# A two-model transformer chain in float32 by split weights: the rows of x handed from block to block in halves, with GpSimd multiplying them by their norm

## What is computed

```python
def first_block(...):
    for l in range(DEPTH):
        mod = cs @ w_ada[l] + b_ada[l]
        h = rmsnorm(x, g_pre[l]) * (1.0 + scale) + shift
        y = hybrid_mixer(h, w_in[l], w_out[l], ...)
        x = x + gate * rmsnorm(y, g_post[l])
def second_block(...):
    for i in range(DEPTH):
        h = _modulate(x, sh_a, sc_a)
        m = _neighborhood_attention(h, ...) if i % 2 == 0 else _mla(h, ...)
        x = x + g_a[:, None, :] * m
        h = _modulate(x, sh_f, sc_f)
        f = _swiglu(h, ...) if i % 2 == 0 else _moe(h, ...)
        x = x + g_f[:, None, :] * f
    return _rmsnorm(x) * final_norm
```

## Time and profile before

| | |
|---|---|
| median of 3 runs | 1661.28 us (1660.46 to 1663.12) |
| profiled execution, device time | 1663.32 us |
| its span in the profile | 1661.5 us, 21232 instructions |
| TensorE matmuls busy | 1427.0 us (86%) |
| VectorE busy | 1216.3 us (73%) |
| ScalarE busy | 862.0 us (52%) |
| GpSimd busy | 65.6 us (4%) |
| chain that ended last | TensorE 53%, VectorE 27%, ScalarE 9% |

### The profile page before, as it was taken

How to read it: one execution, slowest core, us unless ns; L and a number is a source line. 1 busy time by engine, 2 the same in 40 slices (tenths; PEclk the granted TensorE clock), 3 DMA queues, 4 the chain that set the end, 5 groups by cost and what they waited for, 6 DMA issues and landing times.

```text
span 1661.5 us, 21232 instructions
## 1 busy us (share of the span) xinstructions
PE 1427.0 (86%) x7628; PEld 1191.2 (72%) x7628; DVE 1216.3 (73%) x1484; ACT 862.0 (52%) x1210; POOL 65.6 (4%) x82
## 2 busy tenths in 40 slices
PE   2799986999869976899986796999999999999993
PEld 1688676886758845899985685877777777777772
DVE  8667556866565655788785645789889888899895
ACT  0444444444434434233433554577777777776772
POOL 0000000000010000000000102100000000000001
PEclk9989898998989979899997897899999999999996
DMA  9764423735236632678774203699899999999782
GB/s 397 298 249 147 159 101 142 277 142 189 77 143 250 240 128 76 250 279 302 283 276 143 96 38 136 252 350 366 339 347 368 345 349 374 329 365 356 287 371 89
DMA packets 61537, 403.08 MB, mean 243 GB/s; under 512 B 6534, under 2 KB 9734, under 8 KB 15116
## 3 DMA queue, kind: packets, MB, share of 16 engines
q1 hardware_dynamic: 52416, 379.45, 60.3%
q10 hardware_dynamic: 7020, 15.17, 2.6%
q0 software_dynamic: 2016, 7.34, 1.2%
HBM read 393.01 MB, written 8.91 MB: 242 GB/s over the span
## 4 chain that ended last, share of the span: by engine, by line
PE 53%; DVE 27%; ACT 9%; issue 7%; DMA 2%; POOL 1%; ACTq 0%; DVEq 0%; SPq 0%; POOLq 0%
DVE w_lo L2177 16%; PE PS L826 14%; PE PS L828 13%; PE PS L827 13%; ACT w_hi L1602 4%; ACT xg L1696 2%; DVE acc L2194 2%; PE PS L998 1%; PE PS L978 1%; DMA raw<-in_ws 1%; DVE a_lo L2337 1%; DVE hb L2346 1%; DVE hb L2348 1%; PE PS L1251 1%; PE PS L896 1%
## 5 line engine op out<-in xcount | busy, mean ns | idle before, releaser
L2177 DVE TENSOR_TENSOR w_lo<-raw,w_hi 128x2048 fp32r<-128x2048 f32 x287 | 659.6, 2298 | 160.8 <-ACT w_hi L1602 138.3
L1602 ACT ACTIVATE w_hi<-raw 128x2048 fp32r<-128x2048 f32 x287 | 547.8, 1919 | 234.9 <-PE PS L828 222.2
L826 PE MATMUL PS<-w_hi,h_hi 128*128 128x512 f32 (+2 forms) x812 | 340.2, 419 | 28.6 <-DVE h_lo L2598 8.9
L827 PE MATMUL PS<-w_lo,h_hi 128*128 128x512 f32 (+2 forms) x812 | 321.3, 396 | 0.0
L828 PE MATMUL PS<-w_hi,h_lo 128*128 128x512 f32 (+2 forms) x812 | 321.2, 396 | 0.0
L826 PE MATMUL PS<-h_hi,w_hi 128*128 128x256 f32 x776 | 232.3, 299 | 21.4 <-DVE h_lo L2222 11.4
L827 PE MATMUL PS<-h_lo,w_hi 128*128 128x256 f32 x776 | 224.3, 289 | 0.0
L828 PE MATMUL PS<-h_hi,w_lo 128*128 128x256 f32 x776 | 224.1, 289 | 0.0
L826 PEld LDWEIGHTS PS<-w_hi,h_hi 128*128 128x128 f32 x812 | 157.9, 194 | 73.8 <-DVE w_lo L2177 15.7
L2194 DVE SCALAR_TENSOR_TENSOR acc<-raw,cs,acc 128x512 f32<-128x512 f32 x252 | 189.5, 752 | 8.9
L828 PEld LDWEIGHTS PS<-w_hi,h_lo 128*128 128x128 f32 x812 | 157.7, 194 | 33.7
(11 more groups left out here) (310 smaller groups left out, 1444.9 us busy)
## 6 DMA issues: line engine op xcount, KB each, us to landing
raw<-in_ws SPq DMA_DIRECT2D x359, 1024.0 KB, 5.6
y_rows<-ysb ACTq DMA_DIRECT2D x10, 512.0 KB, 7.4
rp<-in_rp ACTq DMA_DIRECT2D x8, 384.0 KB, 4.7
ckb<-in_ck ACTq DMA_DIRECT2D x2, 1024.0 KB, 4.9
y_rows<-ones ACTq DMA_DIRECT2D x3, 512.0 KB, 8.6
x<-in_x SPq DMA_DIRECT2D x1, 1024.0 KB, 11.6
gpost<-in_gpost ACTq DMA_DIRECT2D x2, 512.0 KB, 5.2
x_rows<-xn_f ACTq DMA_DIRECT2D x2, 512.0 KB, 3.8
```

Source lines behind the costliest of these rows:

```text
L826: t.matmul(out, lhs[0], rhs[0], start=start, stop=False, skip_group_check=True)
L827: t.matmul(out, lhs[0], rhs[1], start=False, stop=False, skip_group_check=True)
L1602: a.activation(wh[:, SPL_AT[e.phase][i], :], raw[:, r, :], ACT.Copy).then_inc(*e.inc("hi"))
L2177: v.tensor_tensor(wl[:, s, :], raw[:, r, :], wh[:, s, :].bitcast(F32), ALU.subtract).then_inc(*e.inc("raw_used"))
```

## The change

**Halves.** `turn` works on one half. A new function `first_sums` on TensorE does, for half 0 and then for half 1, the transposes and all sums of the first slot of that half; it is used in `lay0`, `lay1`, `na` and `mla`. In `ffn` only the transposes are by halves. ScalarE's and VectorE's `norm` treat half 0 to the end before half 1, with hb in two parts: VectorE scales the first 4 feature tiles of a half, ScalarE the other 4. The update of x at the end of a phase becomes part of the next phase's `norm` (`lay_update`, `sums_update`), so it stands behind that phase's first w_hi and w_lo.

**GpSimd.** It makes the inverse root of each half by itself and then multiplies that half of x by it (`normed`); VectorE's multiplications are gone.

**Order.** So that a first slot can be summed by halves of tokens, the MoBA values become slot 0 of a layer, and the rest move back by one; four slots stand ahead of the ticks now and four in them. `turn_y(0, 1, 5)` moves into `out_moba(0)`. `cmp_out` moves behind `turn_probs`. In `na` the w_ada blocks end before the last two weight blocks, two filling pieces stand ahead of `scores(0)`, and the output sums run in another order, as in `mla` before. In `ffn`, `down` goes by halves, and `ada(11)` stands ahead of the last one.

```diff
-LAY_FILL = [(1, 2) if i % 4 == 3 and i < 16 else (1, 1) for i in range(18)] + [(0, 0)] * (LAY_TICKS - 18)
+LAY_FILL = [(1, 1)] * 14 + [(0, 1)] * 4 + [(0, 0)] * (LAY_TICKS - 18)
-LAY_ADA = {8: 2, 9: 3, 11: 4, 14: 5}
+LAY_ADA = {9: 2, 10: 3, 12: 4, 15: 5}
-NA_FILL = [(1, 2)] * 8 + [(0, 0)] * (NA_TICKS - 8)
-NA_OUT = {10: 1, 11: 1, 12: 1, 13: 1, 14: 1, 15: 1, 16: 2}
+NA_AHEAD = 2
+NA_FILL = [(1, 2)] * 6 + [(1, 1)] * 2 + [(0, 0)] * (NA_TICKS - 8)
+NA_OUT = {9: 1, 10: 1, 11: 1, 12: 1, 13: 1, 14: 1, 15: 2, 16: 2}
...
+            def normed(xn, m):
+                pool.wait_ge(*e.last("rstd"))
+                g.tensor_scalar(xn[:, m, :], x[:, m, :], st[:, s_rs + m:s_rs + m + 1], None,
+                                ALU.mult).then_inc(*e.inc("xn"))
...
+            for p in ("lay0", "lay1", "na"):
+                e.enter(p)
+                for m in range(MT):
+                    if p != "lay0":
+                        rstd(2 * m + 1, [(2 + m, 3 + m, D)])
+                    rstd(m + 1 if p == "lay0" else 2 * m + 2, [(m, m + 1, D)])
+                    normed(xn_n if p == "na" else xn_l, m)
...
+            def turn(src, m):
+                pe.wait_ge(*e.at("xn", m + 1))
...
+            def first_sums(src, banks, width, m0_done=None):
+                for m in range(MT):
+                    turn(src, m)
...
+                    for kh in range(2):
+                        pe.wait_ge(*e.at("hi", kh + 1))
+                        pe.wait_ge(*e.at("h_hi", 2 * m + kh + 1))
...
                     for c in range(2):
+                        if m == 0 and c == 1:
+                            pe.wait_ge(*e.at("y", 4))
+                            turn_y(0, 1, 5)
...
+                if posted:
+                    y_square(xn, 0)
+                square(xn, 0)
+                hi_to(2)
+                if posted:
+                    y_square(xn, 1)
+                elif e.phase != "lay0":
+                    square(xn, 1)
+                if ahead:
+                    ahead()
+                hi(0, 0)
+                scaled(0)
+                hi(0, 1)
+                if posted or e.phase == "lay0":
+                    square(xn, 1)
+                hi_to(SPL)
+                hi(1, 0)
                 scaled(1)
+                hi(1, 1)
...
+                updated(0)
+                if posted:
+                    scaled(0)
+                    updated(1, (0,))
+                    lo(0, 0)
+                    updated(1, (1,))
+                    lo(0, 1)
+                    split_to(2)
...
+                scaled(1)
+                lo(1, 0)
+                lo(1, 1)
+                split_to(SPL)
```

More of the change, by code:

```diff
@@ L62, in lay_steps_before @@
     out = sum(n for t, n in LAY_OUT.items() if t < tick)
-    return 6 + pieces // 4 + (out >= 6) + (out >= 8)
+    return 8 + pieces // 4 + (out >= 6) + (out >= 8)
 def lay_slots_before(tick):
@@ new lines, in out_sums @@
+                def out_sums():
+                    pe.wait_ge(*e.at("h", 5))
+                    for c in range(2):
+                        yield from out_piece(0, 0, c)
+                    pe.wait_ge(*e.at("h", 6))
+                    yield from out_piece(0, 1, 0)
+                    pe.wait_ge(*e.at("h", 7))
+                    for c in range(2):
+                        yield from out_piece(1, 0, c)
+                    yield from out_piece(0, 1, 1)
+                    pe.wait_ge(*e.at("h", 8))
+                    for c in range(2):
+                        yield from out_piece(1, 1, c)
@@ L1318, in neighbourhood @@
                 ada(0)
-                for b in LAY_BANK[0:6]:
+                fill, out = projections(), out_sums()
+                for _ in range(NA_AHEAD):
+                    next(fill)
+                for b in LAY_BANK[1:6]:
                     pe.wait_ge(*e.at(f"bank{b}", 1))
                 scores(0)
-                fill, out = projections(), out_first()
                 for i in range(NA_TICKS):
@@ L1366, in neighbourhood @@
                         values(i - 1)
-                out_second(0)
-                pe.wait_ge(*e.at("o_used", 4))
-                turn_o(1, 5)
-                out_second(1)
+                next(out)
+                turn_o(3, 5)
+                for _ in out:
+                    pass
             neighbourhood()
@@ L2012, in _ @@
             start("ffn")
-            squares(xn_f)
-            get_brow(4)
-            h_hi()
+            norm(xn_f, ahead=lambda: get_brow(4))
             ffn()
```

504 lines of the change are left out of this document (228 added, 276 removed).

## The result

The changed kernel takes 1666.8 us (median of 6 runs, 1661.9 to 1669.7), the kernel before 1661.8 in the same runs: ratio 1.0029, 95% interval 1.0017 to 1.0042.

The account below looks back on a forecast made before the run. TensorE was taken to idle in hand-over chains and in gaps inside blocks. Hand-overs -8.2, layers -4 and neighbourhood attention -10.3 sum to -22.5 us: 1640.8 profiled, 1639 against the median, stated as 1640, range 1627 to 1657.

Parts of the forecast that it names:

- The unknown price: GpSimd's multiply of 128x1024 elements by a column of scalars: taken as 1.5 us, ends 1.0 and 4.75.
- The hand-overs: Five passages between blocks: first layer +0.6, layer 1 -4.9, neighbourhood -4.9, FFN +1, latent attention 0; together -8.2 us.
- the 1.7 us of the transposes: Last transposes of y inside out_moba(0): its 1.48 us wait goes and out_moba(1) ends 1.7 us earlier.
- rival (a): Hand-overs: TensorE stays at its lower clock for both first halves, leaving 4.3 us of gain, 1657; chance 0.13.
- 2.3 comes back: Into the FFN: 20.4 us against 17.0, but w_lo number 1 stood behind it before, so the net loss is 1 us.
- half 1 waits for half 0's sums and ends about where both ended before: Into the latent attention: half 0's first matmul at 898.5 against 902.38, half 1's end unchanged, so 0 us.
- Inside the blocks: Layers: cmp_out's move -4 us; neighbourhood attention: filling pieces, w_ada order, transposes and clock, less 3 lost, -10.3 us.
- -4 for cmp_out: In each layer, a filling piece and transposes now fill the gap ahead of cmp_out: 2.0 us gained each.
- Rival (b): Gaps inside the blocks come back elsewhere; only the hand-overs and the transposes count: 1652 us, chance 0.14.
- (c): GpSimd's multiply costs 4.75 us at about eight places in the hand-over chains: 1665, slower; decides from 4.3; chance 0.09.
- (d): Hand-overs: half 1's chain is so long that half 0 only waits earlier: 1659 to 1663 us, chance 0.07.
- What would show it: Trace signs: multiply 1.3 to 2 us; wrong if multiplies exceed 4, clock low through both halves, or new gaps between ticks.

Follow-up runs that it names:

- dve_a: Changed kernel with VectorE instead of GpSimd multiplying both halves, half 1 behind w_lo: 1649.9 us, ratio 0.9920 to the kernel before.
- ffn_lo: Changed kernel with VectorE multiplying, half 1 ahead of w_lo, but into the FFN w_lo number 1 behind both halves: 1652.2 us, ratio 0.9938 to the kernel before.
- undo_both: Changed kernel with cmp_out back at the head of ticks 6 and 7 and ada(11) behind the last down projection: 1668.6 us, ratio 1.0045 to the kernel before.
- the second execution: Profiled execution of the changed kernel run once more, unchanged: 1666.6 us profiled, median of that run 1667.2 us.
- before_turny: Kernel before with only the last transposes of y moved between the column halves of out_moba(0) in both layers: 1661.6 us, ratio 1.0004.

## Why the prediction was wrong

*The view of what bounds the kernel* was right: the hand-overs are chains that TensorE waits for, and what lengthens them by one microsecond costs it.

*The unknown price* is the step that failed first. I took 1.5 us for GpSimd's multiply, "since both rows read and write as this one does", from the rate of a copy (0.975 ns an element), between ends of 1.0 and 4.75. Measured: 2.85 us, 2.5 ns a column and 0.27 fixed. The row of the same operation, 0.594 for 128 columns, fixes the point at 128; I put the slope of another operation behind it. The page's best case, worked out beside the sum at 1.54 us plus a fixed part (the Trainium skill, GPSIMD Engine Reference, "3.1 Elementwise"), was as low; the measurement decides. By dve_a against the changed kernel, 2.1 us less a multiply gives 17.4 in all, some 8.2 us for each microsecond of it. The rival's eight places in the chain were counted well; with 2.85 for 1.5 they cost 11 us, an estimate. That alone would have left half of the 22.5 us forecast, and the kernel faster.

*The hand-overs*, then, are the second step that failed. Forecast as stages of the table (the 1.7 us of the transposes belongs to the layers there), measured, and what the measured ends (2.85 us, 0.75 us) give at 1.5 us on a straight line between them, an estimate:

| | forecast | changed | dve_a | at 1.5 us |
|---|---|---|---|---|
| into layer 0 | +0.6 | +3.9 to +4.9 | +0.1 | +1.6 |
| into layer 1 | -3.2 | +1.8 | -3.8 | -1.8 |
| into neighbourhood | -3.2 | +0.9 | -3.4 | -1.8 |
| FFN, with the block | +1.0 | +4.5 | +4.2 | +4.3 |
| ada(10) to latent | 0 | +5.0 | +2.2 | +3.2 |
| sum | -4.8 | +16.1 to +17.1 | -0.7 | +5.5 |

The price explains 11 of some 21 us; the last column against the first gives the other 10. Of these, 1.0 lies in the first layer. Behind the layers it is 2.8: rival (a) was partly right, and its place was half 1, not half 0. Counted from the layer's end, half 1's sums were to start at 18.7 us and start at 21.7, of which twice 1.35 is the multiply's; so the chain up to there was right but for the price. They were to take 6.5 us and take 8.6 in the changed kernel: in half 0 the low clock is covered, in half 1 it is not (8.6 us against 5.8 in dve_b), and I had allowed 1 us for it. Into the FFN 3.3: I said of w_lo number 1 that "2.3 comes back" in the block; ffn_lo puts 2.4 us at the hand-over and shows that the place between the halves gives back 1.3 in the block and 0.5 at the last down. The hand-over was to lose 3.4 and lost 5.2 with either engine's multiply (22.21 and 22.16), and against the kernel before only 0.7 came back in the block. Into the latent attention 3.2: "half 1 waits for half 0's sums and ends about where both ended before". It doesn't. First sums start at 892.39, 27.0 us ahead of the landmark, where they stood 19.8 ahead of it: between the halves stand half 1's transposes and the wait for its scaling, 2.23 us at 902.84, in a place where both halves' sums ran on before, and the last down takes 16.1 us from ada(10) for 13.8. I had counted the place of ada(11) there as neutral; at this hand-over it is a gain of 4.2 (undo_both), so what else the change does there loses the more. How much each of the transposes, the wait and the longer last down costs there was not tried by itself.

*Inside the blocks* it held in the main: -17.7 forecast, -14.8 measured in the second execution. With the hand-overs' 21.9 and the rest's 1.1 these 2.9 us come, but for rounding, to the 25.7 us between -22.5 forecast and +3.2. The neighbourhood attention: -10.3 forecast, -9.4 measured, -7.6 alone in the kernel before; its size is partly luck, since the block varies by 4 us between kernels with the same schedule. Layers: -4 for cmp_out and -3.4 for the transposes of y forecast; measured -5.4 in the second execution (-9.5 in the first), 2.6 of it cmp_out's. The transposes of y are not told apart from nothing in the time (before_turny), though the wait is gone. Rival (b) has a share: a new wait of 3.59 us stands at 176.39 for ScalarE's copy of modc and one of 2.98 at 150.32 for VectorE's y, and the change has ticks with a piece fewer in a row of them; that the one causes the other was not tried by itself.

```profile
150.32 0.52 PE L1031 MATMUL PS<-vsw,ptp 128*128 128x64 f32 x2 [2.98 <-DVE y L2638]
...
176.39 0.35 PE L902 MATMUL PS<-ones,acc 128*128 128x1 f32 x2 [3.59 <-ACT modc L1691]
```

*The rivals.* (c), slower through the multiply, is the one that came, at 2.85 us and not from 4.3: its threshold rested on a gain of 22.5 us, of which 10 wasn't there. So its outcome came by half through its own cause. (d) fell: half 0's sums stand ahead and run early. The range's upper end, 1657, was (a) alone; price and hand-over terms were never put together at their bad ends.

*What would show it.* The first sums of layer 1 stand at 264.86, 14.4 us behind the Square that out_moba(0) releases (250.47; 13 were forecast); the waits ahead of half 1's sums are 1.25 and 2.23 us (3 to 5 in all); the root step beside w_lo takes 1.72 us (some 2), and the 6.91 us gap is gone. Two signs said wrong: the multiply, outside its 1.3 to 2 us though not above 4, and the waits of 2.98 and 3.59 us inside the layers that were not there before. A low clock stands at the start of both halves' sums, not through them.

## What to carry to other kernels

An operation's price on a slow engine is read from a row of that operation in two sizes, or tried by itself; the slope of a copy says nothing of it. An engine that is free is no cheaper for a step on a chain that TensorE waits for: count the step's place in the chain, not the engine's load. The clock of the matmuls behind a wait is worth a term with two ends: the same 24 sums took 5.7 us in some kernels and 7.2 to 8.6 in others, and the length of the wait did not tell which. Where a hand-over is cut into halves, the second half pays transposes, scaling and their wait again: with VectorE's multiply it gained 3.4 to 3.8 us behind the layers and lost 4.2 into the FFN, where TensorE waits for both halves, and 2.2 into the latent attention. Compare stages, in more than one execution, before a difference of a few microseconds is given to an edit.
